# Rope pages and query blocks of the sample attention in memory that is free earlier, and its first gathers issued during the new tokens' attention

## What is computed

```python
c_past = cache_kv_latent[i][page_table].reshape(db, past, KV_LORA)
kr_past = cache_k_rope[i][page_table].reshape(db, past, ROPE_DIM)
q_abs = einsum('bthn,chn->bthc', q_nope, w_uk)
s_past = einsum('bthc,bsc->bhts', q_abs, c_past) + einsum('bthr,bsr->bhts', q_rope, kr_past)
s_new = einsum('bthc,buc->bhtu', q_abs, c_new) + einsum('bthr,bur->bhtu', q_rope, kr_new)
p = softmax(concat([s_past, s_new]) * scale)
o_lat = einsum('bhts,bsc->bthc', p[..., :past], c_past) + einsum('bhtu,buc->bthc', p[..., past:], c_new)
```

## Time and profile before

| what | us |
|---|---|
| median of 3 runs | 1027.24 |
| the runs | 1026.8, 1027.24, 1029.7 |
| the profiled execution | 1029.6 |
| its span, first to last instruction | 1027.7 |
| TensorE busy in the span | 974.2 (95%) |
| DVE busy | 666.5 (65%) |
| ACT busy | 387.2 (38%) |
| POOL busy | 39.1 (4%) |

### The profile page before, as it was taken

How to read it: one execution, slowest core, us unless ns; L and a number is a source line. 1 busy time by engine, 2 the same in 40 slices (tenths; PEclk the granted TensorE clock), 3 DMA queues, 4 the chain that set the end, 5 groups by cost and what they waited for, 6 DMA issues and landing times.

```text
span 1027.7 us, 22122 instructions
## 1 busy us (share of the span) xinstructions
PE 974.2 (95%) x9086; PEld 898.9 (87%) x9086; DVE 666.5 (65%) x1054; ACT 387.2 (38%) x857; POOL 39.1 (4%) x44
## 2 busy tenths in 40 slices
PE   4899999999999999599999999999999999999995
PEld 3899999988888897455569999999999999999995
DVE  7467556765555555888837658697774335767567
ACT  4234332324151514333323323556661124565331
POOL 0000000000000011333100000000000000000000
PEclk9899999999999999899999999999999999999998
DMA  9504444313233324999643934224323243341643
GB/s 256 169 24 106 122 122 108 89 23 102 50 96 85 105 102 158 383 344 354 243 161 118 281 85 125 82 82 115 90 82 93 81 114 83 94 111 56 190 119 124
DMA packets 174772, 136.88 MB, mean 133 GB/s; under 512 B 18707, under 2 KB 162936, under 8 KB 170328
## 3 DMA queue, kind: packets, MB, share of 16 engines
q1 hardware_dynamic: 166442, 93.47, 32.5%
q0 software_dynamic: 5760, 37.75, 9.8%
q10 hardware_dynamic: 2502, 4.68, 1.2%
HBM read 124.18 MB, written 11.80 MB: 132 GB/s over the span
## 4 chain that ended last, share of the span: by engine, by line
PE 78%; DVE 12%; issue 4%; ACT 3%; DMA 1%; ACTq 0%; DVEq 0%; another core or an unknown queue 0%; POOL 0%; POOLq 0%
PE PS L2014 34%; PE PS L2242 8%; PE PS L2694 8%; PE PS L2756 6%; PE PS L2025 3%; PE PS L2471 3%; DVE w_lo L1225 2%; PE PS L2589 2%; PE PS L2414 2%; ACT p_sample L972 2%; PE PS L2279 1%; PE PS L2268 1%; PE PS L2340 1%; DVE y_tok L1734 1%; PE PS L2256 1%
## 5 line engine op out<-in xcount | busy, mean ns | idle before, releaser
L2014 PE MATMUL PS<-x_hi,w_hi 128*128 128x262 f32 (+1 forms) x744 | 164.0, 292 | 2.7 <-DVE x_lo L1272 1.4
L1225 DVE TENSOR_TENSOR w_lo<-w_raw,w_hi 128x2048 fp32r<-128x2048 f32 (+3 forms) x65 | 125.9, 1937 | 59.7 <-ACT w_hi L703 48.2
L2014 PE MATMUL PS<-x_lo,w_hi 128*128 128x262 f32 (+1 forms) x744 | 160.0, 287 | 0.0
L2014 PE MATMUL PS<-x_hi,w_lo 128*128 128x262 f32 (+1 forms) x744 | 159.6, 286 | 0.0
L703 ACT ACTIVATE w_hi<-w_raw 128x2048 fp32r<-128x2048 f32 (+3 forms) x59 | 94.5, 1601 | 145.9 <-PE PS L2014 88.3
L2014 PEld LDWEIGHTS PS<-x_hi,w_hi 128*128 128x128 f32 x744 | 120.7, 190 | 6.0 <-issue 2.4
L2014 PEld LDWEIGHTS PS<-x_lo,w_hi 128*128 128x128 f32 x744 | 120.1, 190 | 0.0
L2014 PEld LDWEIGHTS PS<-x_hi,w_lo 128*128 128x128 f32 x744 | 120.0, 190 | 0.0
L2242 PE MATMUL PS<-x_hi,w_hi 128*128 128x262 f32 (+1 forms) x256 | 78.7, 307 | 0.0
L2242 PE MATMUL PS<-x_hi,w_lo 128*128 128x262 f32 (+1 forms) x256 | 73.3, 286 | 0.0
L2242 PE MATMUL PS<-x_lo,w_hi 128*128 128x262 f32 (+1 forms) x256 | 73.3, 286 | 0.0
(11 more groups left out here) (376 smaller groups left out, 2293.2 us busy)
## 6 DMA issues: line engine op xcount, KB each, us to landing
w_raw<-in_w_ffn_in_dram SPq DMA_DIRECT2D x44, 512.0 KB, 4.5
w_raw<-in_w_in_dram SPq DMA_DIRECT2D x37, 512.0 KB, 6.7
w_raw<-in_w_ffn_out_dram SPq DMA_DIRECT2D x28, 320.0 KB, 3.8
w_raw<-in_w_o_dram SPq DMA_DIRECT2D x12, 512.0 KB, 5.2
w_raw<-in_w_ffn_out_dram SPq DMA_DIRECT2D x16, 384.0 KB, 3.9
gate_scratch<-gate_out ACTq DMA_DIRECT2D x8, 524.0 KB, 2.9
gates<-gate_scratch SPq DMA_DIRECT2D x8, 524.0 KB, 9.0
x_T_scratch<-x_sum_T SPq DMA_DIRECT2D x1, 2144.0 KB, 7.5
```

The source lines that it names most:

```text
L1225: V.tensor_tensor(WL[:, at_, ks], RAW[:, at_, ks], WH[:, at_, ks].bitcast(F32), ALU.subtract).then_inc(s_wsplit, 1)
L2014: last = T.matmul(PS[:, bank, 0:n], w[:, par, kw + k, m * P:(m + 1) * P], x[:, k0 + k, half * n:(half + 1) * n], start=start and k == 0 an ...
```

## The change

Memory: `q_blocks` leaves `gate_out` and gets a place of its own behind `w_uv`. `pages_r` and what follows it begin at 66208 instead of 65536, so that the half of `pages_r` for even samples lies where nothing is during the last head pair. The others (`p_sample`, `rope_T`) still lie on `gate_out`.

POOL: rope_page(0) is issued right behind pair (0,6). Pairs (1,0) and (1,4) are issued at probs_ready 38, pairs (1,2) and (1,6) at 40, before attn_done; rope_page(1) after attn_done.

ACT: `spread_query` does not wait for the gate store any more; the wait stands behind `stage_query(0)`, ahead of the copy of a weight slot.

DVE: the memset of the PSUM columns (L1635) comes before the three chunks and raises `rows_set` by itself, so TensorE can start on it; the memset of `p_sample` stays behind the gate store and is the second count, for which TensorE waits at its first `weigh_chunk`. Later waits for `rows_set` count one more.

```diff
-        (_, CTX, QAB, UV), e3b = plan(e3, ("gap5", [P, 392]), ("c_tok0", [T0, KVL]), ("q_abs", [P, 2, DEC, HEADS]), ("w_uv", [P, 2, 512]))
+        (CTX, QAB, UV), e3b = plan(e3, ("c_tok0", [T0, KVL]), ("q_abs", [P, 2, DEC, HEADS]), ("w_uv", [P, 2, 512]))
...
-        (PGR, PB, SSM, OL, SPART, OPART, QBD, RTT), e4 = plan(
-            65536, ("pages_r", [P, 2, NPAGES, ROPE]), ("p_sample", [P, 2, 36, HEADS]),
+        (PGR, PB, SSM, OL, SPART, OPART, RTT), e4 = plan(
+            66208, ("pages_r", [P, 2, NPAGES, ROPE]), ("p_sample", [P, 2, 36, HEADS]),
             ("sm", [P, 2, 48]), ("o_lat", [P, 2, HEADS, DEC]),
-            ("score_parts", [P, 2, P]), ("out_parts", [P, 2 * KVL]), ("q_blocks", [P, 2, 9, 32]),
+            ("score_parts", [P, 2, P]), ("out_parts", [P, 2 * KVL]),
             ("rope_T", [P, 4, NCH, 32]))
+        QBD = at("q_blocks", e3b, [P, 2, 9, 32])
...
@@ POOL
                 chunk_pair(0, c)
+            rope_page(0)
+            pool.wait_ge(S["out_stored"], 16 * 7)
+            pool.wait_ge(S["probs_ready"], 6 * NT + NCH)
+            chunk_pair(1, 0)
+            chunk_pair(1, 4)
+            pool.wait_ge(S["probs_ready"], 8 * NT)
+            chunk_pair(1, 2)
+            chunk_pair(1, 6)
             attn_done = Count(S["attn_done"], start=1)
             pool.wait_ge(attn_done.sem, attn_done.after(4))
-            pool.wait_ge(S["out_stored"], 16 * 7)
-            rope_page(0)
-            for b in range(1, DEC):
+            rope_page(1)
+            for b in range(2, DEC):
...
                     if c == 2:
-                        if b >= 2:
-                            pool.wait_ge(S["rope_turned"], b - 1)
+                        pool.wait_ge(S["rope_turned"], b - 1)
                         rope_page(b)
@@ ACT
             def spread_query():
-                for j in range(2):
-                    act.wait_ge(stored[j].sem, stored[j].after(1))
...
             spread_query()
             stage_query(0)
+            for j in range(2):
+                act.wait_ge(stored[j].sem, stored[j].after(1))
             hi(N_MERGE + 1, 4)
@@ DVE
             dve.wait_ge(attn_done.sem, attn_done.after(4))
+            V.memset(PS[:, 6, 256:264], NEG).then_inc(S["rows_set"], 1)
             for c in range(EARLY, 4):
                 turn_chunk(0, c)
             for j in range(2):
                 dve.wait_ge(S[f"gate_stored{j}"], 16 * (1 + 4))
-            V.memset(PS[:, 6, 256:264], NEG)
             V.memset(PB[:, :, 33:36, :], 0.0).then_inc(S["rows_set"], 1)
@@ TensorE, weigh_chunk
                 if c == 0:
+                    if b == 0:
+                        pe.wait_ge(S["rows_set"], 2)
```

More of the change, by code:

```diff
@@ L275, in build @@
         assert NCH * 1024 * 4 <= 2 * KT * COLS * 4
-        assert e4 + 8 * KVL * 4 <= e3 + 392 * 4
+        assert e4 + 8 * KVL * 4 <= e3
         def page(b, c):
@@ L1015, in _ @@
             outputs_back(DEC - 1)
-            act.wait_ge(S["rows_set"], 2)
+            act.wait_ge(S["rows_set"], 3)
             for k in (slice(0, 2), slice(2, 4)):
@@ L1072, in _ @@
             product, w_sum = Count(S["sum_product"]), Count(S["sums_ready"], start=4)
-            act.wait_ge(S["rows_set"], 3)
+            act.wait_ge(S["rows_set"], 4)
             def conv_start(m, f):
@@ L2567, in _ @@
             pe.wait_ge(ab.sem, ab.after())
-            pe.wait_ge(S["rows_set"], 2)
+            pe.wait_ge(S["rows_set"], 3)
             merge_tile(N_MERGE + 2, 0, range(2))
```

## The result

| what | before, us | after, us |
|---|---|---|
| median of 8 runs each | 1027.02 | 1032.9 |
| lowest and highest | 1026.22, 1029.7 | 1032.25, 1039.37 |
| the profiled execution | 1029.6 | 1039.37 |
| its span | 1027.7 | 1037.1 |

The ratio is 1.006, with an interval of 1.0037 to 1.0083: the change makes the kernel 5.9 us slower. The forecast was 1024.0 and its range ended at 1027.3. The profiled execution of after is the slowest of its eight, so each place is read against the issue of its own gate store.

A forecast was written before the change was run, and what follows sets the result against it. DVE was taken to set the sample attention's start, TensorE and ACT its cycle. Gains of 1.0 (store) + 2.3 (remote wait) = 3.3 us took 1029.6 to 1026.3; less 2.4 for the median, 1023.9, told as 1024.0; range 1021.8 to 1027.3.

The forecast's parts named there:

- the time of the gate store, 414.4: Store seen at 414.4, so DVE's rope transpose starts at 414.5, not 415.53: 1.0 us gained.
- the bound of 417.2: Latest start of DVE's rope transpose, if the gate store goes last in the queues: 1.7 us lost.
- The alternation by packet: Gathers, weights and gate store were assumed to take turns packet by packet on the DMA engines, giving the store's time.
- the wait of 2.29 us: DVE's wait before scores_back at 428.07, read as TensorE's instructions late through a full queue; whole 2.3 us gained, bounds 0 and 2.3.
- rival (a): The remote wait before scores_back stays: only 1.0 us gained, 1026.2 us; chance 0.20.
- so the shift goes through to the end: The 3.3 us gained at L2441 last to the kernel's end, since no wait in the later TensorE and ACT cycle was for pages.
- The wait for the rope pages: DVE's 2.28 us wait before the rope transpose at 415.53 goes, since rope page 0 is gathered early.
- the first scores: TensorE's first score matmuls start at 412.9 instead of 415.74, which alone gains nothing at the end.
- ACT's copy behind the store: ACT's 1.06 us copy after the gate store ends at 415.5 (late case 418.2), hidden before TensorE needs the parts at 420.2.
- (d): Slower: weight packets mixed with gathers move slowly, store lands at 422.5, 1031.9 us; decided by a transpose after 420.9; chance 0.08.
- (b): The gate store is not slowed: 2.2 + 2.3 = 4.5 us gained, 1022.7 us; chance 0.15.
- (c): The gate store goes last in the queues: 2.3 - 1.7 = 0.6 us gained, 1026.6 us; chance 0.12.

The follow-up runs named there:

- rope1_behind: The changed kernel with the gather of rope page 1 issued only behind the gate store; 1020.8 us, ratio 1.0018 to the kernel before.
- weights_behind: The changed kernel with the last merge weights loaded behind the gate store and copied after sample 0's new-token step; 1033.7 us, ratio 1.0048 to the kernel before.
- sp_gathers2: Repeat run: the kernel before with sample 2's pages fetched by SyncE in plain transfers instead of POOL's gathers; 1023.88 us, ratio 0.9963.
- wait_s_full: The kernel before with POOL held at pair (2,2) until TensorE has added sample 0's new-token score; 1021.49 us, ratio 1.001.
- B: A further measuring occasion on one chip, not known to differ from the first; the kernel before had a median of 1019.17 us there.
- A: A further measuring occasion on one chip, not known to differ from the first; the kernel before had a median of 1028.85 us there.
- C: A further measuring occasion on one chip, not known to differ from the first; the kernel before had a median of 1027.49 us there.

## Why the prediction was wrong

**The step that failed first: the time of the gate store, 414.4, from which the forecast took a rope transpose at 414.5 and 1.0 us gained.** The transpose came at 418.13; with the store issued as late as before it would be 419.1, beyond even the bound of 417.2. Three inputs were wrong. The store was taken to begin 2.2 us after its issue; its first packet moved 3.6 us after it, as in every profile with the two pairs in front (3.6 to 3.8; 1.4 to 2.0 in all others). Its passage was taken as 4.0 us (409.8 to 413.8) and took 7.4: the forecast gave the store about 21% of the engines and then 74%, and in the stretches 410 to 412, 412 to 414 and 414 to 416 it had 12.4, 26.5 and 29.1%. And rope page 1, issued at 408.54, was not counted beside the store, neither in the sum nor in the bound, although its issue is part of the same change; rope1_behind prices it at about 1.6 us of the passage. That the weights would be the lesser part was right (1.5 us). The alternation by packet, from which the passage was worked out, shows from 412 to 414 (92, 97, 96), but not everywhere (in weights_behind 86 to 190 from 413 to 415, and the counts of 410 to 412 in the kernel before, 245, 179 and 20, are not one for one either). The rule of the Trainium skill ("DMA: Bandwidth & Descriptors", section "Queues, rings and completion order") holds in 412 to 414, and the store's late beginning isn't explained by it; why it begins late stays open.

**The second: the whole 2.3 us taken as gained, for the wait of 2.29 us.** It was read as instructions fetched late through a full queue, from one instruction packet in a stretch of 97.1% gathers. sp_gathers2 refutes it: full queue, no wait. The wait comes with POOL's issues (a TensorE semaphore held during them, as theory P reads it), and it stayed, 3.27 us long, since in the changed kernel too POOL issues back to back when chunks 0 to 3 of sample 1 are turned, which is when sample 0's scores are ready. The rule of the Trainium skill that was set against the reading ("Runtime: NRT & Kernel Launch", section "Instruction fetch mechanics": crossing a block is mostly hidden) agrees with that: no stall of this kind shows, and rival (a), whose condition was that this wait stays, was right in this.

**The third: "so the shift goes through to the end".** The first cycle took 15.29 us for 13.19. The forecast had no term for the clock. In stretches of 2 us of the changed kernel and of weights_behind:

```profile
434.00:436.00 2.00, 2.00 (x34) 1.53 (x30) 2.00 (x2) 0.79 (x6) 0.00 (x0) 0.50 0.55 225
436.00:438.00 2.00, 1.72 (x30) 1.21 (x22) 2.00 (x3) 1.79 (x14) 0.94 (x1) 0.50 0.00 0
```
```profile
436.00:438.00 2.00, 1.10 (x26) 0.72 (x22) 2.00 (x2) 1.81 (x14) 0.94 (x1) 1.00 0.36 57
```

In the changed kernel TensorE idled for 4.02, 2.79, 3.04 and 0.79 us between 415.4 and 432.4. Its clock was at the lower level (1.2 GHz) three times: from 412 to about 415, from about 418.5 to 428.7, and, after a stretch at 1.00 from 430 to 432, again from 432 to about 442, so that most of the first cycle ran at half clock. In the kernel before the clock falls at the same place, but for a shorter time: the stretch 434 to 436 is at 1.00 again, after one at 0.50 and one at 0.85. weights_behind is as late but is back at 1.00 from 436, and its first cycle is 13.41: so most of the 2.1 us belong to this long third stretch and not to the late store as such. Both profiles of the changed kernel have such a first cycle (15.29 and 15.00), and so has wait_s_full on B, where the store was not late (15.13, from 426.68 to 441.81, with the clock at 0.50 from 428 to 436); the other kernels with holds have 13.2 to 14.5. Why the lower clock lasts longer there isn't settled.

**What was right.** The wait for the rope pages went; the first scores started at 411.95, 5.3 us behind the store's issue (forecast: 412.9, 5.3); that this alone gains nothing; ACT's copy behind the store (418.05 to 419.11) is hidden ahead of parts_back at 420.13; POOL's early issues delay nobody on POOL; from the second cycle on, undisturbed cycles took 13.3 to 13.4 us.

**The rivals.** (d) had the sign and the mechanism, a store behind gathers mixed with small packets, but at the wrong size: the store was seen at 418.1, not 422.5. Its deciding point, a transpose later than 420.9, supposed that the 2.3 us were gained. Without them the point is 415.53 + 3.1 = 418.6, and the transpose came at 419.1 on the scale of before. So in this profile it took both failed steps to reach the border of slower, and the clock to pass it clearly. (a) was right that the wait stays, (b) fell, and (c) fell too, though its late store was nearer than the forecast's.

## What to carry to other kernels

Before you issue a transfer earlier, list what is issued just behind it on every queue and who waits for that; here 2.1 MB that nobody needed yet went ahead of a 0.5 MB store that DVE and the second half of the scores waited for, and the same pairs issued from 2 us behind the store on cost nothing. Take the beginning of the queued transfer and its passage as two unknowns; here both were too short in the forecast. And a wait whose releaser the profile can't name should not enter a forecast at its whole value until an experiment has moved it: look first at what other engines are doing at its end.

## What the runs showed of the hardware

**TensorE semaphores and POOL's gather issues.** On all occasions but B (the first, A and C) a TensorE semaphore due during the issue of an indirect gather (0.94 us) was often seen late. Where issues follow each other 0.3 us apart, it was seen 0.85 to 1.10 us after the end of an issue, and the chain of them made 2.7 to 3.4 us of it. For a semaphore due during a single issue or just behind it, it was less: 0.43 to 0.52 us after the issue's end (in the changed kernel the half ends at 437.44, the issue at 437.37, and ACT goes on at 437.87), and where the semaphore was due in the first 0.2 us of a single issue, it was seen some 0.4 us late, still within the issue (419.46 and 419.90 in the kernel before, issue from 419.30 to 420.24). On B there was none of this.

The undisturbed cycle is 13.2 to 13.4 us where there are holds, and 11.9 us on B (449.07 to 461.00 in rope1_behind), and the kernel before is 8 us faster there (1019.17 against 1027.49), about six times the difference of a cycle; that the holds make all of that difference was not tested. In such a cycle of the kernel before the spread of the maxima ends at 443.52, within an issue (442.67 to 443.61), and ACT, which waits for it, goes on at 444.60, 1.08 us later; in rope1_behind on B it goes on 0.04 us behind it (450.59, 450.63). But not every TensorE semaphore is held: the turn of the maxima in the kernel before ends at 442.20, within the issue of 441.43 to 442.37, and DVE goes on at 442.24. Which are held, and why chips differ, stays open.

**A store behind gathers.** With two gathers of 1.05 MB issued just ahead of it, the 0.5 MB store moved its first packet 3.6 to 3.8 us after its issue, against 1.4 to 2.0 us, and was seen after 11.4 us, against 5.1 to 6.5 us in the kernels that issue the two pairs behind it. SyncE's issue of two weight transfers took 6.61 us in the same stretch, for 1.05.
